# Sharing the low-part splits of a projection between engines in a two-layer attention kernel

## The reference

```python
def dsa_sparse_attention(h, pos, w_in, w_out):
    proj = h @ w_in
    q, k, v, qi, ki, wi = jnp.split(proj, B_SPLITS, axis=-1)
    ...                                    # partial rotary on q, k, qi, ki
        logits = jnp.einsum('bthd,bsd->bths', qi_blk, ki)
        score = jnp.einsum('bths,bth->bts', jax.nn.relu(logits), wi_blk)
        _, idx = lax.top_k(score, n_sel)   # n_sel = 128, causal keys only
        ...                                # softmax over the kept keys, times v
    return out @ w_out
for layer in range(DEPTH):
    hn = rmsnorm(x, g[0])                  # g[0] is a gain for each of the 1024 features
    x = x + rmsnorm(mix(hn), g[1])
    x = x + rmsnorm(squared_relu_mlp(rmsnorm(x, g[2]), w_up, w_down), g[3])
```

## Time and profile before

| | |
|---|---|
| time, median of 3 runs (lowest, highest) | 1079.87 us (1077.4, 1080.5) |
| the profiled execution: time, span in its trace | 1078.13 us, 1076.3 us |
| mean granted TensorE clock | 0.997 |
| TensorE busy | 1056.6 us (98%) |
| VectorE busy | 747.4 us (69%) |
| ScalarE busy | 538.3 us (50%) |
| GpSimd busy | 192.7 us (18%) |
| chain that ended last | TensorE 88%, VectorE 5%, DMA 3%, ScalarE 1% |

### The profile page before, as it was taken

The page is one execution under the profiler, slowest core; times in us unless marked ns, Lnnn a source line. Parts: engine busy times, 40 slices in busy tenths (PEclk is TensorE's granted clock), DMA queues, the critical chain, the costliest instruction groups (busy, mean ns, idle before and its releaser), DMA issues.

```text
span 1076.3 us, 14866 instructions
## 1 busy us (share of the span) xinstructions
PE 1056.6 (98%) x5408; PEld 859.0 (80%) x5408; DVE 747.4 (69%) x1284; ACT 538.3 (50%) x1016; POOL 192.7 (18%) x335
## 2 busy tenths in 40 slices
PE   9999999999999999999999999999999999999997
PEld 8777779888888888888778766679888888888885
DVE  5455536586697697687579898526596696696684
ACT  6677545353453443425554567645254444453422
POOL 0465320000000000005403387520000000000005
PEclk9999999999999999999999999999999999999999
DMA  9531505645545445332623333006553535535502
GB/s 294 121 79 40 118 1 119 135 88 109 101 95 118 97 99 118 90 68 51 135 43 79 79 79 79 1 1 140 116 111 85 118 81 116 117 79 118 110 9 78
DMA packets 52009, 99.94 MB, mean 93 GB/s; under 512 B 4704, under 2 KB 4832, under 8 KB 51936
## 3 DMA queue, kind: packets, MB, share of 16 engines
q1 hardware_dynamic: 51216, 98.61, 40.9%
q10 hardware_dynamic: 720, 0.38, 0.1%
HBM read 96.88 MB, written 2.10 MB: 92 GB/s over the span
## 4 chain that ended last, share of the span: by engine, by line
PE 88%; DVE 5%; DMA 3%; ACT 1%; issue 1%; SPq 1%; POOL 0%; POOLq 0%; DVEq 0%; ACTq 0%
PE bank L2038 11%; PE bank L2039 11%; PE bank L2037 11%; PE bank L2397 7%; PE bank L2398 7%; PE bank L2396 7%; PE bank L2047 6%; PE bank L2049 5%; PE bank L2048 5%; PE bank L2186 3%; PE bank L2421 3%; PE bank L2420 3%; PE bank L2422 3%; PE bank L2255 2%; DMA w_raw<-in_a_w_in 2%; PE bank L2241 2%
## 5 line engine op out<-in xcount | busy, mean ns | idle before, releaser
L2037 PE MATMUL bank<-r_hi,w_hi 128*128 128x512 f32 (+1 forms) x456 | 177.5, 389 | 0.0
L2038 PE MATMUL bank<-r_hi,w_lo 128*128 128x512 f32 (+1 forms) x456 | 177.4, 389 | 0.0
L2039 PE MATMUL bank<-r_lo,w_hi 128*128 128x512 f32 (+1 forms) x456 | 177.4, 389 | 0.0
L1636 DVE TENSOR_TENSOR w_lo<-w_raw,w_hi 128x1024 fp32r<-128x1024 f32 x84 | 102.0, 1222 | 71.3 <-ACT w_hi L1165 71.2
L1165 ACT ACTIVATE w_hi<-w_raw 128x1024 fp32r<-128x1024 f32 x84 | 87.8, 1056 | 120.2 <-PE bank L2039 82.9
L2396 PE MATMUL bank<-w_hi,hid_hi 128*128 128x512 f32 x336 | 130.7, 389 | 0.0
L2397 PE MATMUL bank<-w_lo,hid_hi 128*128 128x512 f32 x336 | 130.7, 389 | 0.0
L2398 PE MATMUL bank<-w_hi,hid_lo 128*128 128x512 f32 x336 | 130.7, 389 | 0.0
L810 POOL TENSOR_TENSOR acc<-acc,G 128x512 f32<-128x512 f32 x8 | 13.0, 1650 | 594.3 <-ACT waste L1024 594.3
L1174 ACT ACTIVATE w_hi<-w_raw,gT 128x512 fp32r<-128x512 f32 x96 | 64.5, 715 | 106.0 <-DMA w_raw<-in_w_mlp_up 74.6
L2037 PEld LDWEIGHTS bank<-r_hi,w_hi 128*128 128x128 f32 (+1 forms) x456 | 85.2, 187 | 18.2
(11 more groups left out here) (213 smaller groups left out, 2149.4 us busy)
## 6 DMA issues: line engine op xcount, KB each, us to landing
w_raw<-in_w_mlp_up SPq DMA_DIRECT2D x64, 512.0 KB, 6.5
w_raw<-in_w_mlp_down SPq DMA_DIRECT2D x64, 512.0 KB, 7.0
w_raw<-in_b_w_in SPq DMA_DIRECT2D x16, 512.0 KB, 6.8
w_raw<-in_a_w_in SPq DMA_DIRECT2D x8, 512.0 KB, 9.1
w_raw<-in_a_w_out SPq DMA_DIRECT2D x8, 512.0 KB, 5.8
w_raw<-in_b_w_out SPq DMA_DIRECT2D x8, 512.0 KB, 6.0
xt<-in_x_turned SPq DMA_DIRECT2D x8, 256.0 KB, 5.7
X<-in_x SPq DMA_DIRECT2D x4, 512.0 KB, 11.2
```

What stands on the lines that cost most here:

```text
L1636: nc.vector.tensor_tensor(half_of(w_lo[:, u % 2, :], a), b_of(PRODUCTS[i][1], a), half_of(w_hi[:, u % 2, :], a).bitcast(f32), ALU.subtract ...
L2037: nc.tensor.matmul(bank, whi, xhi, start=start, stop=False)
L2038: nc.tensor.matmul(bank, wlo, xhi, start=False, stop=False)
L2039: return nc.tensor.matmul(bank, whi, xlo, start=False, stop=stop)
```

## The change

Four things are changed, all in layer 1.

1. *Units 56, 58 and 59.* ScalarE multiplies the pieces `k` = 2 and 3 by their gain in the raw buffer itself (`rescale`), ahead of the split; their high part is then a plain copy. VectorE writes the low part only of pieces 0 and 1. GpSimd writes that of pieces 2 and 3 by plain subtraction (`rest_low`). TensorE and the load that reuses the buffer wait for both.
2. *Unit 61.* It is no longer shared: ScalarE writes both high halves, VectorE the whole low part in one subtraction of 2048 columns.
3. *The last two query tiles*, 17 and 18, are transposed into a dense bank rather than into the banks of the probabilities; TensorE waits for the bank to have been read.
4. *Rounds of top-k.* 14 rather than 11 rounds of block 2 stand before attention; the tables for the turns are shifted to match.

```diff
-POOL_UNITS = (60, 61, 62, 63)
-
-SHARED = 61
+POOL_UNITS = (60, 62, 63)
+
+RESCALED = (56, 58, 59)
...
+def q_bank(layer, qn):
+    return d_bank(layer, d_no(1, "out", 1, 0)) if last_queries(layer, qn) else t_bank(layer, ("q", qn))
...
             def load(u, src):
                 sp.wait_ge(*low_of(u - 2))
+                if u - 2 in RESCALED:
+                    sp.wait_ge(*rest_of(u - 2))
...
+            def rest_low(u):
+
+                w_h, w_l = w_place(u)
+                whole = raw(RAW[u][0])
                 for k in (2, 3):
                     cs = slice(512 * k, 512 * k + 512)
+                    pool.wait_ge(*((w_hi_part, part_hi_no(u, 2)) if k == 2 else (w_hi_done, hi_no(u))))
+                    nc.gpsimd.tensor_tensor(w_l[:, cs], whole[:, cs], w_h[:, cs].bitcast(f32), ALU.subtract).then_inc(in_lo_done, 1)
...
+            def rescale(u):
+
+                whole = raw(RAW[u][0])
+                act.wait_ge(*loaded(u))
+                for k in (2, 3):
+                    cs = slice(512 * k, 512 * k + 512)
+                    nc.scalar.activation(whole[:, cs], whole[:, cs], ACT.Copy, scale=gain(1, 0, 4 * half_no(u) + k)).then_inc(rescaled, 1)
...
+                        if u in RESCALED and k >= 2:
+                            act.wait_ge(rescaled, 2 * RESCALED.index(u) + k - 1)
+                            last = nc.scalar.activation(w_h[:, cs], whole[:, cs], ACT.Copy)
...
-            split(56)
+            split(56, (0, 1))
...
-            top_rounds(2, 1)
+            top_rounds(2, 2)
             q_low(1, 11)
-            top_rounds(2, 4)
-            split(58)
+            top_rounds(2, 5)
+            split(58, (0, 1))
             q_low(1, 12)
-            top_rounds(2, 6)
-            split(59)
+            top_rounds(2, 8)
+            split(59, (0, 1))
...
-            ROUNDS_2 = (11, 12, 13, 14, 15, TOPK // 8)
-            ROUNDS_3 = (0, 1, 2, 3, 4, 5, 6, 8, 10, 12, 14, TOPK // 8)
+            ROUNDS_2 = (14, 14, 14, 15, TOPK // 8)
+            ROUNDS_3 = (0, 0, 1, 2, 4, 5, 6, 8, 10, 12, 14, TOPK // 8)
...
                 if j == 0 and ks[0] == 0:
                     pe.wait_ge(*low_of(u))
+                    if u in RESCALED:
+                        pe.wait_ge(*rest_of(u))
...
             def queries_turned(layer, qn):
-                bank = t_free(layer, ("q", qn))
+                if last_queries(layer, qn):
+                    bank = banks[q_bank(layer, qn)]
+                    pe.wait_ge(q_out, q_no(1, 2, 3) + 1)
+                    if qn == q_no(1, 2, 3):
+                        pe.wait_ge(q_lo_done, q_no(1, 2, 2) + 1)
+                else:
+                    bank = t_free(layer, ("q", qn))
```

More of the change, by code:

```diff
@@ L184, in q_no, with last_queries @@
     return 4 * (c - 1) + j if not layer else 7 + 4 * c + j
+def last_queries(layer, qn):
+    return layer and qn in (q_no(1, 2, 2), q_no(1, 2, 3))
 def d_no(layer, what, a, j):
@@ L208, in t_order @@
         order += pts[:2]
-        order += [("q", q_no(layer, c, j)) for c, j in Q_TURN[layer].get(n, ())]
+        order += [("q", q_no(layer, c, j)) for c, j in Q_TURN[layer].get(n, ()) if not last_queries(layer, q_no(layer, c, j))]
         order += [("h", 2 * layer + 1, j, h) for j in H_TURN[layer].get(n, ()) for h in range(2)]
@@ L522, in part_hi_no, with rest_of @@
             return 3 * PIECED.index(u) + k + 1
+        def rest_of(u):
+            return in_lo_done, 2 * RESCALED.index(u) + 2
         def low_of(u):
@@ L879, in _ @@
                     rope_q(10)
[L880 to L883, removed]
+                    rope_k(1, 0)
+                    rope_k(1, 1)
+                    rest_low(56)
+                    rope_k(1, 2)
+                    rope_k(1, 3)
+                    rope_q(11)
+                    rope_q(12)
+                    rest_low(58)
+                    rope_q(13)
+                    rope_q(14)
+                    rest_low(59)
+                    rope_q(15)
+                    rope_q(16)
                 else:
@@ L976, in split @@
                         cs = slice(512 * k, 512 * k + 512)
-                        last = nc.scalar.activation(w_h[:, cs], whole[:, cs], ACT.Copy,
-                                                    scale=gain(layer, 2 if name[:3] == "mlp" else 0, 4 * half_no(u) + k))
+                        if u in RESCALED and k >= 2:
+                            act.wait_ge(rescaled, 2 * RESCALED.index(u) + k - 1)
+                            last = nc.scalar.activation(w_h[:, cs], whole[:, cs], ACT.Copy)
+                        else:
+                            last = nc.scalar.activation(w_h[:, cs], whole[:, cs], ACT.Copy,
+                                                        scale=gain(layer, 2 if name[:3] == "mlp" else 0, 4 * half_no(u) + k))
                         if u in PIECED and k < 3:
@@ L1109, in attention @@
                     for u in SPLITS[layer].get(n - 1, ()) if n > 0 else ():
-                        if u in HALVED and u != SHARED:
+                        if u in HALVED:
                             split_half(u, 1)
@@ L1334, in _ @@
                 relued(X_)
+            rescale(56)
             k_high(1, 1)
@@ L1395, in split @@
                     dve.wait_ge(w_hi_done, hi_no(u))
-                if u == SHARED:
-                    nc.vector.tensor_tensor(w_l[:, 0:1024], whole[:, 0:1024], w_h[:, 0:1024].bitcast(f32), ALU.subtract).then_inc(shared_lo, 1)
-                    return
                 if name[:3] == "out" or name[:3] == "mlp" and mlp_role(layer, u)[0] == "down":
@@ L2031, in d_free @@
                         pe.wait_ge(q_out, 11 + old - 28 + 1)
+                        if d == d_no(1, "out", 1, 0):
+                            pe.wait_ge(q_lo_done, q_no(1, 2, 3) + 1)
                     else:
```

35 lines of the change are left out of this document (13 added, 22 removed).

## The result

| | before | changed |
|---|---|---|
| median of 8 executions each | 1078.41 us | 1082.41 us |
| lowest, highest | 1077.40, 1080.50 | 1080.98, 1086.19 |
| ratio, 95% interval | | 1.0036 [1.0026, 1.0045] |
| executions with a mean granted clock of 0.996 or more | 29 of 35 (beside experiments 5 to 8) | 3 of 8 |
| profiled execution | 1078.13 us, clock 0.997 | 1086.19 us, clock 0.993 |

The account below looks back on a forecast made before the run. TensorE was taken as the bound, with the split of unit 61 fixing its matmul at 652.80. Unit 61 2.7 us late gave 1078.13 + 2.7 = 1080.8, or 1082.5 on the median; range 1076.0 to 1085.3.

Parts of the forecast that it names:

- Splits: Units 56, 58, 59: VectorE and GpSimd subtractions exclude each other, so the splits save VectorE nothing, 0.2 us late.
- Start of attention: VectorE reaches the first masked scores 3.2 us late: three rounds 3.75, splits 0.2, less 0.7 of idle.
- Turn 3: A mask of block 2 (0.36) and a second round of block 3 (1.50) delay turn 5's masked scores by 1.86 us.
- masked scores of turn 4 are 2.1 late: VectorE's lag leaving turns 0 to 2: 3.2 us late on entering, only 1.1 walked out as caught up.
- the main case: Whole kernel: 2.7 us slower, 1082.5 on the median; own range −0.1 to +3.9; chance 0.42.
- masked 5: VectorE's start on the masked scores of turn 5: 3.95 us late, at 630.05 instead of 626.11.
- the matmul of 652.80: TensorE's matmul at 652.80, fixed by unit 61 through the load of unit 63: 2.7 us late, at 655.5.
- Unit 61: VectorE's whole low part of unit 61 is done at 641.1 rather than 638.40, 2.7 us late.
- The dense bank: Last two query tiles: the 1.0 us wait at 633.80 goes, but worth nothing beyond the walk, at best 1.0.
- The two engines seldom meet: Rival: VectorE's quarters fall between GpSimd's, saving 1.37 us a unit; unit 61 is 0.85 early; 1079.0; chance 0.22.
- The relief reaches TensorE: Rival: relief in turns 0 to 2 brings probabilities in time, 3.9 us saved, 1076.0; chance 0.15.
- The clock falls again: Rival: TensorE runs 640 to 643 at half speed behind the gap at 639.4, 4.4 us slower, 1084.3; chance 0.21.

Follow-up runs that it names:

- experiment 5: Changed kernel with GpSimd's six subtractions for units 56, 58 and 59 cut to 4 columns instead of 512, all waits kept: 1079.05 us, ratio 1.0003.
- experiment 6: Changed kernel with the second round of block 3 in turn 3 put back behind the masked scores of turn 5: 1079.42 us, ratio 1.0016.
- experiment 7: Kernel before with only unit 61 whole on VectorE and the last query tiles through the dense bank: 1078.59 us, ratio 0.9999.
- experiment 8: Changed kernel with 16 and 24 extra identity transposes on TensorE ahead of its waits for probabilities of turns 0 and 5: 1080.96 us, ratio 1.0021.
- experiment 2: Changed kernel with units 56, 58 and 59 split as before, VectorE writing all four low parts, no rescaling: 1081.66 us, ratio 1.0027.
- experiment 1: Changed kernel with the top-k rounds of before, 11 rounds of block 2 ahead of attention and the old tables: 1079.93 us, ratio 1.0012.
- experiment 4: Changed kernel with the last two query tiles transposed into the banks of the probabilities as before: 1081.20 us, ratio 1.0022.
- experiment 9: Kernel before with 24 extra identity transposes on TensorE ahead of its wait for the probabilities of turn 2: 1078.11 us, ratio 1.0003.

## Why the prediction was right, and where its sizes were off

**Splits.** Right in the main: VectorE saves 0.5 us in all on units 56, 58 and 59, where 4.1 was what full overlap would give and nothing was forecast. What the earlier trace rows showed elsewhere in the program held at all three units, and experiments 2 and 5 bear it out. The steps behind it were a little too dear: unit 57 was to start 0.85 late and unit 59 1.5; in the changed kernel they were 0.2 and 0.5.

**Start of attention.** VectorE was to enter the first masked scores 3.2 us late; 610.69 − 605.47 − 3.22 = 2.0. The three rounds cost 3.75 as put, but 1.4 of it fell on idle time of VectorE (two waits for ScalarE, which the change's trace no longer has) where I allowed 0.7, and the splits saved 0.5 where I had put 0.2 more.

**Turn 3.** The mask and the second round were to add 1.86 between the masked scores of turns 4 and 5; they added 2.0, and putting one round back returned 1.5 (experiment 6). Right.

**The term that was mis-sized** is the lag with which VectorE comes out of turns 0 to 2: "masked scores of turn 4 are 2.1 late". In the changed kernel they start at 628.05, 628.05 − 621.06 − 3.22 = 3.8 late. The rest is TensorE's clock: 6.6 us at half speed from 615, through the step of the projection behind which the scores of turn 3 stand (VectorE idles 3.65 us for them). Experiment 8, the change with only the transposes added, shows it: with full clock there the lag is 1.0 in its profile. So the 2.1 was about 1 too dear for a clock that holds, and the fall, which the main case had at nothing, added 2.7. In experiment 2, where the clock held too, the same lag is 1.5, masked 5 is 3.4 late (3.95 put), the reciprocal 3.0 (3.6) and the matmul of 652.80 2.0 (2.7). There every term comes out a little below the sum.

**Unit 61.** From masked 5 to the reciprocal: 8.58 us against 8.75 worked out. From there to the end of unit 61: 2.36 against 2.4. Right; added up, the prediction's own terms give 641.2 and 2.8 late, not 641.1 and 2.7. Of the two ways from there to the matmul of 652.80, the one through TensorE's own queue carried the lag in this execution: low outputs 5.9 late where 4.15 was put, 1.5 of waits fallen away where 1.45 was put. The step that needs them is the first output step and not the third. That unit 61 fixes that matmul does not hold by itself: it is done 0.2 late in experiment 1 and 0.3 early in 7, and the matmul is 3.0 and 1.0 late, behind the waits of 3.1 for the low outputs. Not foreseen: VectorE's whole unit blocks GpSimd. Its four multiplications of turn 6 beside it, in GpSimd's timeline:

```profile
638.50 2.33 POOL L807 TENSOR_TENSOR probs<-probs,small 128x256 f32<-128x256 f32 x4 [2.97 <-DVE small L1523]
...
643.95 4.29 POOL L807 TENSOR_TENSOR probs<-probs,small 128x256 f32<-128x256 f32 x4 [1.61 <-DVE small L1523]
```

**The dense bank.** The 1.0 us wait went. That nothing came of it, as put, is not shown: experiment 4 is unclear.

**The rivals.** "The two engines seldom meet" fell: they met every time. "The relief reaches TensorE" fell too: the waits for probabilities rose from 2.2 to 3.0 us. "The clock falls again" came true beside the main case rather than instead of it: at 642.4, behind the gap at 641, as described, and at 615, which I had not put down, in place of the fall at 619. Its condition, a gap of about 1.7, was wrong: the fall at 615 stands behind waits of 0.51 and 1.15. It is a matter of executions: three of eight held 0.996 and had a median of 1081.2, which is +2.8, near the main case; the other five had 1082.9, +4.5, near this rival's 4.4. The measured 4.0 lies between, 0.1 past the main case's own range (−0.1 to +3.9) and past the 3.2 us where I had drawn the line between no change and slower, with the smaller chance (0.32) on that side.

One valuation of the clock was wrong: I took the half clock in the kernel before to cost 1.7 us. Experiment 9 took it away and won nothing that can be measured.

The Trainium skill's "SBUF — State Buffer", section "Who interferes with whom", names TENSOR_SCALAR among the instructions that can contend though they read one tensor, when its operands meet certain conditions. The mask's 2.04 us beside 0.36 agree with "can"; the 0.36 and 0.45 beside GpSimd's multiplications show that it does not always.

## What to carry to other kernels

Before half of a VectorE instruction's work is given to GpSimd, look in the trace for a place where both already run elementwise instructions on SBUF at once, and see whether either is longer there than alone; if so, expect the halves to run largely one after the other. Work of VectorE that was not longer beside GpSimd here was a subtraction with one operand in PSUM (0.66 us at 624.30 in the kernel before) and a search (MAX8 of 384 columns, 0.55 at 624.87), both beside GpSimd's multiplications from 624.46 to 626.79. When work is moved ahead on the promise of such a saving, time the move without the saving: here that was +2.7 of the 4.0 us. And a stretch at half clock need not cost what it takes away: in the kernel before it cost nothing that can be measured (experiment 9), in the change 1 to 2 us (8). Fill the idle time and see before counting it.

## What the runs showed of the hardware

- A VectorE instruction with one input, the mask (TENSOR_SCALAR, 128x384), waited up to 1.7 us beside GpSimd in two executions (2.04 and 2.02 us), through several of GpSimd's instructions, and hardly or not at all in two others (0.36 and 0.45). Between single subtractions of 512 columns the two engines mostly took turns: 3.53 to 3.63 us for two of each.
- GpSimd is held up the other way round for nearly as long: beside 2.26 us of VectorE's subtract, four multiplications took 4.29 instead of 2.33.
- Nearly identical waits of TensorE (0.5 and 1.15 us) were followed by 1.2 GHz in the profiled execution of the change and not in that of experiment 2. Executions of one kernel with a lower mean clock took 1.7 us more and above (medians 1081.2 and 1082.9 in the change, 1079.2 and 1083.7 in experiment 6). With transposes of the identity in the idle time the mean granted clock was 0.996 or more in 44 of 44 executions of four kernels, though not at 1.0 throughout.
